# Joining the two probability maps of a head before they are turned, in the second block's attention

## The reference

```
scores = jnp.einsum('bqhmd,bkhmd->bhmqk', qb, kh)
mask = k_pos[None, :] <= q_pos[:, None]
p = jax.nn.softmax(jnp.where(mask, scores, -jnp.inf), axis=-1)
w = p[:, :, 0] - lam * p[:, :, 1]
return jnp.einsum('bhqk,bkhd->bqhd', w, vf)
```

## Time and profile before

| | |
|---|---|
| Runs of the kernel before | 2359.89 us median of 3 (2359.66 to 2361.32) |
| Span of the profiled execution | 2357.0 us |
| What the median has beyond that span | 2.89 us (2359.89 - 2357.0); the profiled execution has no other time of its own than its span |
| TensorE busy | 2318.0 us, 98% |
| VectorE busy | 1455.3 us, 62% |
| ScalarE busy | 1305.4 us, 55% |
| GpSimd busy | 334.5 us, 14% |

### The profile page before, as it was taken

One profiled execution on the slowest core, in us unless ns is written; L12 is line 12 of the kernel. 1 busy time (PEld: TensorE's weight loads), 2 busy tenths in 40 slices (PEclk: granted clock), 3 DMA queues, 4 the chain that ended last, 5 costly groups with the idle time before them and its releaser, 6 DMA issues.

```text
span 2357.0 us, 36716 instructions
## 1 busy us (share of the span) xinstructions
PE 2318.0 (98%) x15344; PEld 2077.0 (88%) x15344; DVE 1455.3 (62%) x2209; ACT 1305.4 (55%) x1958; POOL 334.5 (14%) x307
## 2 busy tenths in 40 slices
PE   7999999999999999999999999999999999999999
PEld 6799978888899888998789988899899898998998
DVE  6654555546654546556764577576687676765875
ACT  5554465555644556445564467464665675655654
POOL 0100032212100413001010003333000022530000
PEclk9999999999999999999999999999999999999999
DMA  6255543333455534555245544344455453444553
GB/s 266 90 213 182 181 175 143 142 128 125 180 196 183 194 142 163 186 196 201 100 179 190 186 176 159 137 155 164 177 195 182 174 184 126 168 155 161 199 195 125
DMA packets 58181, 398.93 MB, mean 169 GB/s; under 512 B 6816, under 2 KB 7072, under 8 KB 11680
## 3 DMA queue, kind: packets, MB, share of 16 engines
q1 hardware_dynamic: 56864, 393.75, 46.0%
q10 hardware_dynamic: 1152, 2.83, 0.3%
HBM read 395.51 MB, written 1.05 MB: 168 GB/s over the span
## 4 chain that ended last, share of the span: by engine, by line
PE 89%; DVE 5%; ACT 4%; issue 1%; POOL 0%; DMA 0%; SPq 0%; ACTq 0%; DVEq 0%; POOLq 0%
PE b L1281 14%; PE b L1283 13%; PE b L1282 13%; PE b L1179 12%; PE b L1180 12%; PE b L1181 12%; PE b L1184 6%; PE b L1188 4%; DVE wlo L1929 2%; ACT b L1575 1%; ACT whi L1579 1%; PE b L1247 1%; PE b L1248 1%; DVE xb L2225 1%; PE b L1257 0%
## 5 line engine op out<-in xcount | busy, mean ns | idle before, releaser
L1929 DVE TENSOR_TENSOR wlo<-raw,whi 128x2048 fp32r<-128x2048 f32 x362 | 843.6, 2335 | 449.4 <-ACT whi L1579 449.1
L1579 ACT ACTIVATE whi<-raw 128x2048 fp32r<-128x2048 f32 x362 | 690.4, 1912 | 429.9 <-PE b L1283 233.6
L1281 PE MATMUL b<-xh,whi 128*128 128x256 f32 x2560 | 723.9, 283 | 0.6
L1283 PE MATMUL b<-xh,wlo 128*128 128x256 f32 x2560 | 712.6, 278 | 0.0
L1282 PE MATMUL b<-xl,whi 128*128 128x256 f32 x2560 | 712.0, 278 | 0.0
L1281 PEld LDWEIGHTS b<-xh,whi 128*128 128x128 f32 x2560 | 480.4, 188 | 5.3 <-DVE wlo L1929 2.8
L1282 PEld LDWEIGHTS b<-xl,whi 128*128 128x128 f32 x2560 | 481.4, 188 | 1.9
L1283 PEld LDWEIGHTS b<-xh,wlo 128*128 128x128 f32 x2560 | 481.2, 188 | 0.0
L1179 PE MATMUL b<-whi,xh 128*128 128x512 f32 x640 | 262.9, 411 | 1.4 <-DVE wlo L1929 1.4
L1179 PE MATMUL b<-whi,oh 128*128 128x512 f32 x656 | 259.0, 395 | 0.6 <-DVE ol L2216 0.6
L1180 PE MATMUL b<-wlo,oh 128*128 128x512 f32 x656 | 256.1, 390 | 0.0
(11 more groups left out here) (237 smaller groups left out, 2931.5 us busy)
## 6 DMA issues: line engine op xcount, KB each, us to landing
raw<-in_w SPq DMA_DIRECT2D x362, 1024.0 KB, 4.8
gt<-in_rows SPq DMA_DIRECT2D x8, 512.0 KB, 4.0
bt<-in_rows SPq DMA_DIRECT2D x8, 512.0 KB, 4.9
abq<-in_rows ACTq DMA_DIRECT2D x2, 768.0 KB, 6.3
x<-in_x SPq DMA_DIRECT2D x1, 1024.0 KB, 6.5
bc<-in_rows SPq DMA_DIRECT2D x4, 256.0 KB, 5.3
out<-x SPq DMA_DIRECT2D x4, 256.0 KB, 2.3
msk<-in_masks SPq DMA_DIRECT2D x1, 768.0 KB, 21.3
```

Of the source, the lines that this page charges most:

```text
L1281: pe.matmul(out, wh[:, k, cs], ah[:, kk, :], start=kk == 0 and s == 0, stop=False, skip_group_check=True)
L1283: last = pe.matmul(out, wl[:, k, cs], ah[:, kk, :], start=False, stop=final and k == 3, skip_group_check=True)
L1579: return ac.activation(out, i, ACT.Copy)
L1929: ve.tensor_tensor(B.wlo[r][:, :], B.raw[r][:, :], B.whi[s][:, :], ALU.subtract).then_inc(sem["loV"], 1)
```

## The change

`probs` and `pv` of the second block's attention work on one map instead of two. A new step, `join`, stands in the list ahead of `score`: VectorE takes the reciprocals and lam as `differ` did, multiplies the second map S1 (128 and 256 columns, one share for each tile of queries) in place in SBUF, and then forms S0 times its share minus S1, also in place. TensorE waits for the semaphore `joined`, turns the joined map, ScalarE alone copies it to `PT[0]`, and `pv` writes the two tiles' results to banks 4 and 5. `differ` is gone; `joined` copies the two results to `og`. The turned map uses banks 6 and 7 by turns.

```diff
@@ -517,7 +517,7 @@
 
         return a + v // 4, v % 4
 
-    def attention(self, a, n, mask, ready, consume, kidx, dv, sinks=None, tail=None, pace=7, values=None, weigh=None, before=None):
+    def attention(self, a, n, mask, ready, consume, kidx, dv, sinks=None, tail=None, pace=7, values=None, weigh=None, before=None, layer=None):
 
 
 
@@ -532,10 +532,13 @@
                 tail(due.pop(0)[0])
             for i in range(2):
                 self.bank(("S", a, v, i), SB[i])
-                if 1 <= v <= n or v >= 2 and dv == 128:
-                    self.bank(("T", a, v, i), TB[i])
+                if 1 <= v <= n and (dv == 64 or i == 0):
+                    self.bank(("T", a, v, i), TB[i if dv == 64 else v % 2])
             if v >= 2:
                 self.step("pv", a, v - 2, dv, n)
+            if dv == 128 and 1 <= v <= n:
+                self.counts("joined", (a, v - 1))
+                self.step("join", a, v - 1, layer)
             if v < n:
                 if sinks is not None:
                     self.counts("filled", (a, v))
@@ -551,13 +554,9 @@
             if v >= 2 and sinks is not None:
                 consume(v - 2)
             if 1 <= v <= n:
-                for i in range(2):
-                    if v >= 2 and dv == 128:
-                        sem = ("copied_a", "copied_v")[i]
-                        self.counts(sem, (a, v - 1))
-                        self.copied[a, v - 1, i] = (sem, self.mark[sem, (a, v - 1)])
-                    else:
-                        self.copied[a, v - 1, i] = (f"empty{TB[i]}", self.use["T", a, v, i][1] + 1)
+                for i in range(2 if dv == 64 else 1):
+                    b, m = self.use["T", a, v, i]
+                    self.copied[a, v - 1, i] = (f"empty{b}", m + 1)
                 self.step("probs", a, v - 1)
             if v < n:
                 self.step("exp", a, v, sinks is not None)
@@ -1019,8 +1018,8 @@
                 yield
 
             def consume(g):
-                self.step("differ", u, g, l)
-            yield from self.attention(u, 4, "mc", lambda u: True, consume, lambda v, k: v, 128)
+                self.step("joined", u, g)
+            yield from self.attention(u, 4, "mc", lambda u: True, consume, lambda v, k: v, 128, layer=l)
             yield from self.head_norm(("sub", u), "yo", 6)
             self.counts("yog", u, 2)
             self.step("subscale", u, l)
@@ -1367,10 +1366,14 @@
             mm(B.bank[b][:, 128:384], q[r, p_, 128:256], k[r, at, 0:256], True, True).then_inc(sem[f"full{b}"], 1)
 
     def probs(a, v_):
-        for i in range(2):
+        joined = KIND[a] == "d"
+        for i in range(1 if joined else 2):
             b, n = use["T", a, v_ + 1, i]
             S = B.S[2 * (v_ % 2) + i]
-            p.wait_ge("exp", mark["exp", (a, v_, i)])
+            if joined:
+                p.wait_ge("joined", mark["joined", (a, v_)])
+            else:
+                p.wait_ge("exp", mark["exp", (a, v_, i)])
             p.wait_ge(f"empty{b}", n)
             for k, c in enumerate((0, 129, 257)):
                 last = tr(B.bank[b][:, 128 * k:128 * k + 128], S[:, c:c + 128])
@@ -1383,31 +1386,30 @@
             bv, nv = use["tok", vkey, t]
             p.wait_ge(f"empty{bv}", nv + 1)
         v = B.v[B.slot(a)]
+        if KIND[a] == "d":
+            p.wait_ge(*o.copied[a, v_, 0])
+            pt, c = B.PT[0], 128 * p_
+            for t in range(2):
+                b, n = use["S", a, v_ + 2, t]
+                p.wait_ge(f"empty{b}", n)
+                out = B.bank[b][:, 384:512]
+                last = mm(out, pt[:, 128 * t:128 * t + 128], v[:, 0, c:c + dv], True, t == 0)
+                if t:
+                    last = mm(out, pt[:, 256:384], v[:, 1, c:c + dv], False, True)
+                if v_ + 2 >= pairs:
+                    last.then_inc(sem[f"full{b}"], 1)
+            return
         for i in range(2):
             b, n = use["S", a, v_ + 2, i]
             p.wait_ge(*o.copied[a, v_, i])
             p.wait_ge(f"empty{b}", n)
-            if KIND[a] == "a":
-                c = 64 * (v_ // 2)
-            else:
-                c = 128 * p_ if KIND[a] == "d" else 128 * p_ + 64 * i
+            c = 64 * (v_ // 2) if KIND[a] == "a" else 128 * p_ + 64 * i
             pt, out = B.PT[i], B.bank[b][:, 384:512]
-            last = mm(out[:, 0:dv], pt[:, 0:128], v[:, 0, c:c + dv], True, True)
-            if dv == 128:
-                if v_ + 2 >= pairs:
-                    last.then_inc(sem[f"full{b}"], 1)
-                b, n = use["T", a, v_ + 2, i]
-                p.wait_ge(f"empty{b}", n)
-                out = B.bank[b][:, 384:512]
-                mm(out, pt[:, 128:256], v[:, 0, c:c + dv], True, False)
-                last = mm(out, pt[:, 256:384], v[:, 1, c:c + dv], False, True)
-                if v_ + 1 == pairs:
-                    last.then_inc(sem[f"full{b}"], 1)
-            else:
-                mm(out[:, 64:128], pt[:, 128:256], v[:, 0, c:c + dv], False, False)
-                last = mm(out[:, 64:128], pt[:, 256:384], v[:, 1, c:c + dv], False, True)
-                if v_ + 2 >= pairs:
-                    last.then_inc(sem[f"full{b}"], 1)
+            mm(out[:, 0:dv], pt[:, 0:128], v[:, 0, c:c + dv], True, True)
+            mm(out[:, 64:128], pt[:, 128:256], v[:, 0, c:c + dv], False, False)
+            last = mm(out[:, 64:128], pt[:, 256:384], v[:, 1, c:c + dv], False, True)
+            if v_ + 2 >= pairs:
+                last.then_inc(sem[f"full{b}"], 1)
 
     def opart(key, source):
         i, blk = key
@@ -2408,28 +2412,29 @@
         v.wait_ge("own_v", i)
         ve.tensor_scalar(B.y[:, t, :], B.y[:, t, :], s[:, 27:28], None, ALU.mult).then_inc(sem["yn"], 1)
 
-    def differ(u, g, l):
-        s = g % 2
+    def join(u, g, l):
+
+        s, S0, S1 = g % 2, B.S[2 * (g % 2)], B.S[2 * (g % 2) + 1]
         v.wait_ge("lamv", mark["lamv", l])
-        for kind in "ST":
-            for i in range(2):
-                b, n = use[kind, u, g + 2, i]
-                v.wait_ge(f"full{b}", n + 1)
+        v.wait_ge("exp", mark["exp", (u, g, 1)])
         i = v.mine(ve.reciprocal(B.rl[:, s, 0:4], B.l[u % 4][:, 4 * g:4 * g + 4]))
         v.wait_ge("own_v", i)
         i = v.mine(ve.tensor_scalar(B.rl[:, s, 2:4], B.rl[:, s, 2:4], B.lamt[:, 5:6], None, ALU.mult))
         v.wait_ge("own_v", i)
-        if g < 3:
-            v.wait_ge(*o.copied[u, g + 1, 0])
-        for t in range(2):
-            to = B.og[0][:, t, 128 * g:128 * g + 128]
-            b, n = use["ST"[t], u, g + 2, 1]
-            ve.tensor_scalar(to, B.bank[b][:, 384:512], B.rl[:, s, 2 + t:3 + t], None,
-                             ALU.mult).then_inc(sem[f"empty{b}"], 1)
-            v.wait_ge(f"empty{b}", n + 1)
-            b, n = use["ST"[t], u, g + 2, 0]
-            ve.scalar_tensor_tensor(out=to, in0=B.bank[b][:, 384:512], scalar=B.rl[:, s, t:t + 1], in1=to,
-                                    op0=ALU.mult, op1=ALU.subtract).then_inc(sem[f"empty{b}"], 1)
+        spans = slice(0, 128), slice(129, 385)
+        for t, cs in enumerate(spans):
+            i = v.mine(ve.tensor_scalar(S1[:, cs], S1[:, cs], B.rl[:, s, 2 + t:3 + t], None, ALU.mult))
+        v.wait_ge("own_v", i)
+        for t, cs in enumerate(spans):
+            last = ve.scalar_tensor_tensor(out=S0[:, cs], in0=S0[:, cs], scalar=B.rl[:, s, t:t + 1], in1=S1[:, cs],
+                                           op0=ALU.mult, op1=ALU.subtract)
+        last.then_inc(sem["joined"], 1)
+
+    def joined(u, g):
+        for t in range(2):
+            b, n = use["S", u, g + 2, t]
+            v.wait_ge(f"full{b}", n + 1)
+            ve.tensor_copy(B.og[0][:, t, 128 * g:128 * g + 128], B.bank[b][:, 384:512]).then_inc(sem[f"empty{b}"], 1)
 
     def yparts(l, t, q):
         b, n = use["yturn", l, t, q]
...
@@ -2604,8 +2609,9 @@
     def head_squares(key, buf):
         l = key[1] - 12
         if buf == "yo":
-            b, n = use["T", key[1], 5, 0]
-            g.wait_ge(f"empty{b}", n + 1)
+            for t in range(2):
+                b, n = use["S", key[1], 5, t]
+                g.wait_ge(f"empty{b}", n + 1)
             g.wait_ge("stat_v", mark["stat_v", ("sums", "k", key[1])])
         else:
             for t in range(2):
...
```

More of the change, by code:

```diff
@@ L2474, in vector_program @@
             "build": build, "diag": diag, "mixed": mixed, "ya_lo": ya_lo, "head_roots": head_roots,
-            "head_scale": head_scale, "norm_y": norm_y, "differ": differ, "yparts": yparts, "branch": branch,
+            "head_scale": head_scale, "norm_y": norm_y, "join": join, "joined": joined, "yparts": yparts, "branch": branch,
             "mparts": mparts}
@@ L2833 @@
         "own_v", "own_a", "own_g", "hi", "loV", "loG", "gone", "xhi", "xnv", "xna", "xg", "stat_v",
-        "stat_a", "eps", "tables", "rope", "sinks", "filled", "scored", "exp", "copied_a", "copied_v", "ohi", "merge_g", "silu",
```

(1 more changed line is left out.)

## The result

The changed kernel takes 2372.94 us (median of 4 runs, 2372.55 to 2373.15), the kernel before beside it 2359.77 us (2359.64 to 2361.32): 13.2 us more, ratio 1.0055 with a 95% interval of 1.0041 to 1.0069. It is slower. The predicted time was 2371.3 us, with 2366 to 2377 as the range. The profiled execution of the changed kernel took 2373.15 us, with a span of 2371.3.

What follows compares the result with a forecast made beforehand. TensorE, busy 2318.0 of 2357.0 us, was taken as the bound. Waits of 9.81 less 4.12 saved gave +5.69 a layer, 11.4 for two; span 2368.4 plus 2.9 made 2371.3 us, range 2366 to 2377.

Steps and rivals of the forecast that it cites:

- What is taken from TensorE: Three turns and half the product with the values, 1.03 us a head, 8.24 us less TensorE work over eight heads.
- J: Length of one join on VectorE, from its first instruction to the end of its last, taken as 1.95 us.
- bounds of 1.55 and 2.2: Limits in us for the join's length: four operations started 0.27 apart, or all four dependent; times 2368.4 and 2373.3.
- Round 1: Head 0's turns on TensorE wait for the join, which stands on VectorE behind the branch's operations: 4.06 us.
- The loop: Rounds after the first: each next join hangs on the last turns through ScalarE and VectorE; chains 10.37, 8.95, 11.34 us.
- Round 4: Head 3's turns: chain of 11.34 us against TensorE's own 11.10, a wait of 0.24 us.
- round 2: Head 1's turns: chain of 10.37 us against TensorE's own 7.60, a wait of 2.77 us.
- round 3: Head 2's turns: chain of 8.95 us against TensorE's own 6.21, a wait of 2.74 us.
- The clock rival: TensorE's clock falls to 1.2 GHz behind the new waits; 2376 us taken, chance 0.18.
- main case: TensorE waits for the joins in all four rounds of both layers, slower at 2371.3 us; chance 0.70.
- Not slower: Rival: high and low parts are done ahead of the later joins, only head 0's turns wait; 2359.8 us, chance 0.07.
- faster: Rival: TensorE finds every map joined and never waits; 2351.7 us, chance 0.03.

Runs made afterwards that it cites:

- One map: Changed kernel without the second map or the join; turns wait for the exponentials, the product is scaled by one share: 2351.70 us.
- all waits filled: Changed kernel with dummy turns of the identity ahead of the join waits, 30 before head 0, 15 before heads 1 and 2: 2369.90 us.
- first wait filled: Changed kernel with 30 dummy turns of the identity ahead of head 0's turns only: 2369.84 us.
- first join early: Changed kernel with only head 0's join moved ahead of the low part, two side steps after its exponentials: 2365.60 us.
- changed, again: The changed kernel run once more, unchanged: 2371.76 us.
- longer join: Changed kernel with two more operations in each join, both parts of S1 multiplied by 1.0 in place: 2377.20 us.
- turns and products twice: Changed kernel with each of the three turns and three products with the values issued twice: 2378.53 us.

## Why the prediction was right, point by point

- **What is taken from TensorE, 8.24 us: right.** One map measured 8.0, its stretches 8.1.
- **J = 1.95: 0.16 too long.** Reciprocal and share took 0.46 of the 0.47. The four wide operations took 1.33 (1574.59 to 1575.92), not 1.49. The addition of 0.19 for two of them being 256 wide was right: the groups at the end of this text have 348 against 288 ns and 480 against 351. The mis-sized term is the 1.30 for two pairs as in `differ`. There each pair's second operation waits for its first; in the join both pairs consist of operations that do not wait for each other, so they overlap (0.55 us for 288 and 348 ns, 0.75 for 351 and 480), and only one hand-over lies between the pairs. 1.79 lies inside the bounds of 1.55 and 2.2. The estimate of 1.3, from the row of a table in the Trainium skill (VectorE: DVE Perf Modes, section "The TRN2 errata"), fell short by 0.5. The same section says of that row that it gives too little and puts the measured fixed term at about 150 cycles, not 58; by that the estimate would be about 1.7 (0.47 + 1.23). The measurement decides.
- **Round 1, wait 4.06: measured 3.85.** The place was right to 0.01 us. 0.16 of the difference is J; most of the rest is that the bracket counts from the modelled end of the scores (0.93 us) and the forecast from where the next row can start (0.86).
- **The loop: right in form, 0.2 us too long in each round.** With the clock at 1.00 (all waits filled) the turns of heads 1, 2 and 3 follow at 10.16, 8.74 and 11.14 us; the chain gave 10.37, 8.95 and 11.34. J makes 0.16 of each; the low part reached the join after 2.21 us, not 2.29, for the rest. Round 4's wait of 0.24 is thereby gone: 11.14 is also TensorE's own time there (11.13 in one map). In all the layer comes to +4.96 us instead of +5.69 (40.85 - 35.17 - 0.72), which is +9.9 for two and not +11.4.
- **The wait of round 2, 2.77: it failed in the changed kernel (0.66 and none), and came nearly true where the clock held** (2.46 in first wait filled, with head 0's turns as late as in changed). The join was nearly as late as predicted; TensorE had lost its waiting time to the slow clock before it. By the prediction's own sign, a wait of round 2 or 3 under a microsecond, it was wrong on this point, though the waits of round 3 came (2.44 and 2.43). The 2.81 of first join early is no test of the 2.77: there ScalarE waited 0.35 us more for the row maxima, and the turns came 10.51 us on, not 10.16.
- **The clock rival, given 0.18: its mechanism is real, its size was too large.** Its sign, starts twice as far apart behind the turns, is there (0.21 for 0.12 us). What was measured is thus the main case's loop and the rival's clock together, and the odds of 0.70 to 0.18 had them as alternatives. I took 3.7 us for a fall, with 1.2 left over behind round 1. A fall measured 1.6 and 2.4 us where nothing hid it, and behind round 1 of the changed kernel 0 to 0.36 was left, since the loop hides it. The argument against it, that the waits of rounds 2 and 3 are too short, was wrong: the clock fell after 2.43 us. That one, with no wait behind it, costs 1.5 us (12.62 and 12.64 in place of 11.13) and makes most of the 2.1.

  The trace of before could have shown it. Some 180 us ahead of layer 1's attention, behind two waits of 1.93 and 1.25 us with eight transposes between them, matmuls of 512 columns start 0.43 us apart until 1391.3 and 0.23 apart from there:

```profile
1383.94 1.29 PE L1188 MATMUL b<-cst,xn 128*128 128x128 f32 x8 [1.93 <-DVE xn L2048]
1386.48 0.77 PE L1247 MATMUL b<-whi,xh 128*128 128x512 f32 x1 [1.25 <-issue]
1387.04 0.63 PE L1248 MATMUL b<-wlo,xh 128*128 128x512 f32 x1
1387.46 0.63 PE L1247 MATMUL b<-whi,xh 128*128 128x512 f32 x1
```

  The granted clock is 0.50 there from 1386 to 1391. So the wait of 4.06 was not the only one since the start behind which a fall had to be feared. The Trainium skill has a rule (TensorE: Matmul & The Clock Gate, Part 1) that idleness brings the throttle back. The granted clock of 0.50 behind these waits agrees with it.
- **The rest.** 2371.3 was right to 1.6 us in part by luck, because two errors offset each other: 1.5 us too much for the joins, 2.1 too little for the clock. The median leaves 1.2 us over the stretches' 12.0; changed, again leaves 0.5 over its 11.7. The start of layer 1's stretch moves by up to 2.6 us between profiles, and by 1.6 in the unchanged kernel, so such a rest is of the size of the differences between executions. In the unchanged kernel 1.3 of the 1.6 are the wait for GpSimd at 816.94.
- **Not slower, faster: ruled out** for this order of the list. An earlier join breaks the loop and takes away the wait of round 1 too, and then the "faster" case comes true: 2352.27 and 2351.85 for its 2351.7.

## What to carry to other kernels

Work moved ahead of a busy engine on another engine must be placed by when its inputs are ready, not by when its result is wanted: the same change cost 13 us with the join beside its use and gained 7.5 with the join a round earlier, in idle time. When a wait is added in front of an in-order engine, follow the chain from that engine's next instruction back to the same wait; where it closes, the wait comes again each round. Price a wait on TensorE with the slow clock behind it, and ask what hides that: here it cost at most 0.4 us ahead of another wait, 1.2 to 2.4 us ahead of none.

## What the runs showed of the hardware

The granted clock fell to 0.50, 1.2 GHz, behind each of the twelve unfilled waits of 3.84 to 4.31 us, and matmuls of 256 columns then started 0.21 us apart instead of 0.12, from 1575.98 to 1580.5 in layer 1 and for some 6 us in layer 2. Behind waits of 2.43 to 2.90 us it fell in eight cases (both layers of first join early, of first wait filled and of longer join, layer 2 of changed in two profiles) and held in four (layer 1 of the same two profiles, and the 2.81 and 2.80 of first join early). Behind the 1.76 of turns and products twice it fell in layer 2 and held in layer 1. Behind the pair of waits ahead of layer 1, at 1384 to 1388, it fell in 13 of 14 profiles. So the length of the wait alone does not decide it; what does is open. Turning the identity through the wait held the clock at 1.00, at no cost where the turns ended before the join did. At the program's start the spacing of matmuls and the profile's clock can disagree: in the profile of before matmuls of 512 columns start 0.43 us apart from 19.91 to 22.05 and 0.23 apart from 24.71, and the clock reads 1.00 throughout, so the spacing is to be read beside it.

In-place fp32 operations of VectorE on SBUF took, for 128 and 256 columns, 288 and 348 ns (TENSOR_SCALAR) and 351 and 480 ns (SCALAR_TENSOR_TENSOR), by the groups of the changed kernel:

```profile
L2429 DVE SCALAR_TENSOR_TENSOR S<-S,rl 128x256 f32<-128x256 f32 x8 | 3.8, 480 | 0.0
L2429 DVE SCALAR_TENSOR_TENSOR S<-S,rl 128x128 f32<-128x128 f32 x8 | 2.8, 351 | 0.3
L2426 DVE TENSOR_SCALAR S<-S,rl 128x256 f32<-128x256 f32 x8 | 2.8, 348 | 0.0
L2426 DVE TENSOR_SCALAR S<-S,rl 128x128 f32<-128x128 f32 x8 | 2.3, 288 | 0.3
```

These take their factor from SBUF, one value for each partition. In the longer join the same operation with the constant 1.0 as its factor, right behind the other, took 60 ns less:

```profile
L2429 DVE TENSOR_SCALAR S<-S 128x256 f32<-128x256 f32 x8 | 2.3, 288 | 0.0
L2429 DVE TENSOR_SCALAR S<-S 128x128 f32<-128x128 f32 x8 | 1.8, 228 | 0.3
```
